# Two attention heads side by side, a recurrence that starts from the values, and state-space blocks in pairs: one change to a whole-model kernel

## The reference

```python
# first block, layer 0
m = silu(c) @ w_mod + b_mod                  # 6 D modulation terms from one vector
qkv = silu(depthwise_conv5(p))               # 4 heads of 128
# gated delta rule, forward and backward, over context and then latent tokens:
sol = triangular_solve(lower + eye, [v * b, k * b * exp(gcum)], unit_diagonal=True)
v_new = u - w @ state
state = state * exp(g_last) + k_tail.T @ v_new
o = q_dec @ state + intra @ v_new            # wanted for latent tokens only
# beside it, attention: 8 query heads and 2 key heads of 64, over 512 keys
p = softmax(q @ k.T * 64 ** -0.5); o_b = p @ v
y = concat([rms_norm(o) * silu(z), o_b]) @ w_out
h = h + gate * rms_norm(y);  h = h + gate * rms_norm(swiglu_ffn(h))
# layer 1: a conformer convolution of 31 taps, and a second swiglu_ffn
# second block: three branches of one projection
_, s = associative_scan(combine, (a_bar, B u))       # 32 groups, 64 complex states
y_a = gelu(Re(C s) + d * u);  y_a = y_a * sigmoid(y_a @ w_glu)
y_b = gate_b * causal_conv3(gate_c * x)
y_c = forgetting_attention(q, k, v)                  # 8 heads of 64, decay from f
x = x + rms_norm(sum(sigmoid(gate_i) * (y_i @ w_i)) @ w_out);  then a squared-relu FFN
```

## Time and profile before

| | |
|---|---|
| median of 3 runs | 1442.45 us (1440.03 to 1442.77) |
| the profiled execution | 1443.34 us, of it a span of 1441.4 |
| TensorE (PE) busy | 1338.2 us, 93% |
| VectorE (DVE) busy | 859.3 us, 60% |
| ScalarE (ACT) busy | 480.6 us, 33% |
| GpSimd (POOL) busy | 121.9 us, 8% |
| read from HBM | 223.81 MB, 156 GB/s over the span |

### The profile page before, as it was taken

One profiled execution on the slowest core, in us unless ns is written; L12 is line 12 of the kernel. 1 busy time (PEld: TensorE's weight loads), 2 busy tenths in 40 slices (PEclk: granted clock), 3 DMA queues, 4 the chain that ended last, 5 costly groups with the idle time before them and its releaser, 6 DMA issues.

```text
span 1441.4 us, 18815 instructions
## 1 busy us (share of the span) xinstructions
PE 1338.2 (93%) x7086; PEld 1000.3 (69%) x7086; DVE 859.3 (60%) x1542; ACT 480.6 (33%) x822; POOL 121.9 (8%) x169
## 2 busy tenths in 40 slices
PE   3899968986899999899999999799999999899997
PEld 1564645553488888687488888677777787588886
DVE  1106795443477767496777677378862242577776
ACT  2243235310343343302553443311213230444443
POOL 0041020000000000200000000244530000000000
PEclk9899978998999999899999999999999999999999
DMA  9221244786745553141445555123233233355541
GB/s 393 78 88 45 100 157 176 286 328 233 275 155 182 201 184 133 67 159 44 150 164 202 184 180 196 64 101 131 93 127 110 109 118 106 130 202 178 196 179 59
DMA packets 24655, 225.69 MB, mean 157 GB/s; under 512 B 2705, under 2 KB 2833, under 8 KB 4370
## 3 DMA queue, kind: packets, MB, share of 16 engines
q1 hardware_dynamic: 23040, 220.31, 41.7%
q10 hardware_dynamic: 1554, 4.56, 0.9%
HBM read 223.81 MB, written 1.05 MB: 156 GB/s over the span
## 4 chain that ended last, share of the span: by engine, by line
PE 84%; DVE 7%; DMA 4%; ACT 3%; issue 1%; ACTq 0%; DVEq 0%
PE psum L751 19%; PE psum L829 15%; PE psum L869 14%; PE psum L830 8%; PE psum L782 6%; PE psum L1382 3%; PE psum L914 3%; DMA ring<-in_w_mod 2%; PE psum L734 2%; DMA h<-in_x 2%; PE psum L942 2%; DVE arena L2119 1%; PE psum L1279 1%; PE psum L705 1%; PE psum L1293 1%
## 5 line engine op out<-in xcount | busy, mean ns | idle before, releaser
L829 PE MATMUL psum<-aT_r,arena_r 128*128 128x512 f32 x920 | 327.5, 398 | 0.5 <-DVE arena_r L2020 0.5
L2020 DVE TENSOR_TENSOR arena_r<-ring,arena_r 128x1024 fp32r<-128x1024 f32 x196 | 229.6, 1221 | 129.0 <-ACT arena_r L1489 129.0
L751 PE MATMUL psum<-aT,ring 128*128 128x256 f32 (+1 forms) x1216 | 303.7, 407 | 1.8 <-DVE aT L1983 1.8
L751 PEld LDWEIGHTS psum<-aT,ring 128*128 128x128 f32 x1216 | 229.1, 191 | 70.0 <-issue 42.4
L830 PE MATMUL psum<-aT_r,arena_r 128*128 128x256 f32 x920 | 258.2, 281 | 0.0
L1489 ACT ACTIVATE arena_r<-ring 128x1024 fp32r<-128x1024 f32 x196 | 194.7, 1050 | 161.3 <-PE psum L869 139.1
L869 PE MATMUL psum<-arena_r 128*128 128x512 f32 x912 | 221.9, 392 | 0.0
L829 PEld LDWEIGHTS psum<-aT_r,arena_r 128*128 128x128 f32 x920 | 172.8, 188 | 42.6 <-issue 0.7
L869 PEld LDWEIGHTS psum<-arena_r 128*128 128x128 f32 x912 | 165.9, 188 | 36.4 <-issue 0.3
L830 PEld LDWEIGHTS psum<-aT_r,arena_r 128*128 128x128 f32 x920 | 173.7, 189 | 2.7
L1501 ACT ACTIVATE nrm<-nrm 128x256 f32<-128x256 f32 x76 | 31.8, 418 | 171.1 <-DVE nrm L2034 171.1
(11 more groups left out here) (428 smaller groups left out, 1545.3 us busy)
## 6 DMA issues: line engine op xcount, KB each, us to landing
ring<-in_w_ffn SPq DMA_DIRECT2D x44, 1536.0 KB, 6.6
ring<-in_w_mod SPq DMA_DIRECT2D x32, 1536.0 KB, 7.4
ring<-in_w_ff SPq DMA_DIRECT2D x32, 1024.0 KB, 4.8
ring<-in_w_in_g SPq DMA_DIRECT2D x8, 1536.0 KB, 6.6
ring<-in_w_conf_i SPq DMA_DIRECT2D x8, 1024.0 KB, 4.7
ring<-in_w_hyb_f SPq DMA_DIRECT2D x4, 1536.0 KB, 6.6
ring<-in_w_in_a SPq DMA_DIRECT2D x4, 1536.0 KB, 6.3
ring<-in_w_in_b SPq DMA_DIRECT2D x4, 1536.0 KB, 6.7
```

The lines of the kernel that those rows point to most:

```text
L751: last = mm(bank(use)[:, out_at:out_at + rhs(k).shape[1]], weights[:, k * P:(k + 1) * P], rhs(k), start=(k == 0), stop=(k == KT - 1))
L829: mm(bank(use).rearrange("p (a t) -> p a t", a=2), hi, x_both[:, :, k, :], start=(k == 0), stop=False)
L2020: tt(w_lo[j % 2][:, at], slot(c)[:, at], w_hi[j % 2][:, at].bitcast(F32), ALU.subtract).then_inc(split_ready, 1)
```

## The change

**First attention.** Two heads that share 128 rows form a pair, and there are eight units (`NPAIR`). The two score products of a unit read the upper and the lower 64 rows and go to banks 0 and 1; VectorE takes both maxima in one instruction; the transposes come one unit later, not two; the outputs of both heads are issued in turn into the two column halves of one bank. `att_p` has six buffers, `att_pT` two places. `GAPS` becomes strings, worked from left to right (A: a unit, M: a chunk): one unit stands before the recurrence, the other nine turns in it.

**Ahead of the recurrence.** ScalarE takes both evictions of p5 and of p6, both of q6 and half the diagonal copies (those of GpSimd become four); VectorE keeps the second half of q5 and does the convolution of q behind it. `blocks_inverse` counts in two steps. The chain of v is worked before that of q. At s = 0 `vn` reads v itself, without a copy; q's transposes to tokens move behind the first `vn`, those back to features behind the second, the q by k products behind the second `ds`. `mod_take(2)` moves into the last step. The state S moves to another tile.

**Output projection.** `middle` is called after chunk 0.

**State-space stage.** `s5_in` and `s5_out` take two blocks at a time, their products in turn on neighbouring row groups and column groups. `s5_u` has banks 2 to 5, all projections banks 0 and 1, `s_ri` four buffers; `skip`, `gelu`, `glu_product`, `gated` and `forget` move by one or two places.

```diff
@@ -211,15 +211,16 @@
 USE["att_qk"] = BANKS.turn(3, (0, 1, 2))
 NATT = AH * TT
 USE["att_s"] = BANKS.turn(NATT, (0, 1))
-USE["att_t"] = BANKS.turn(NATT, (2,))
-USE["att_o"] = BANKS.turn(AH // 2, (3,))
-USE["p5"], USE["q5"] = beside(2), beside(2)
+USE["att_t"], USE["att_o"] = [], []
+NPAIR = NATT // 2
+for _n in range(NPAIR + 2):
+    if _n >= 3 and _n % 2:
+        USE["att_o"] += BANKS.turn(1, (3,))
+    if 1 <= _n <= NPAIR:
+        USE["att_t"] += BANKS.turn(2, (2, 3))
+USE["p5"], USE["q5"], USE["p6"] = beside(2), beside(2), beside(2)
 _v = beside(4)
-USE["p6"] = beside(2)
-USE["to_tok"] += beside(2) + _v
 USE["q6"] = beside(2)
-USE["to_feat"] += beside(2)
-USE["kq"] = beside(2)
 for _s in range(4):
     if _s:
         for _d in range(2):
@@ -227,6 +228,12 @@
     for _what in ("vn",) + ("os",) * (_s >= 2) + ("ds",) * (_s < 3) + ("oi",) * (_s >= 2):
         for _d in range(2):
             USE[_what, _s, _d] = beside(1)[0]
+        if (_s, _what) == (0, "vn"):
+            USE["to_tok"] += beside(2) + _v[2:] + _v[:2]
+        elif (_s, _what) == (1, "vn"):
+            USE["to_feat"] += beside(2)
+        elif (_s, _what) == (1, "ds"):
+            USE["kq"] = beside(2)
...
-USE["in_a"] = BANKS.turn(12)
-USE["in_v"] = BANKS.turn(4)
+USE["in_a"] = BANKS.turn(12, (0, 1))
+USE["in_v"] = BANKS.turn(4, (0, 1))

 USE["b_bar"] = BANKS.turn(2, (4, 5))
-USE["in_b"] = BANKS.turn(12)
-USE["in_g"] = BANKS.turn(24)
-USE["s5_u"] = BANKS.turn(S5T, (4, 5))
+USE["in_b"] = BANKS.turn(12, (0, 1))
+USE["in_g"] = BANKS.turn(24, (0, 1))
+USE["s5_u"] = BANKS.turn(S5T, (2, 3, 4, 5))
...
-FORGET = {7: 0, 9: 1, 11: 2, 13: 3, 14: 4, 15: 5}
+FORGET = {7: 0, 9: 1, 11: 2, 14: 3, 15: 4}
...
-    "qk": (2, 1), "p5": (1, 1), "q5": (1, 1), "p6": (1, 1), "q6": (1, 2),
-    "vn0": (2, 2), "ds0": (2, 2), "ks1": (2, 2), "vn1": (2, 2), "ds1": (2, 2),
-    "ks2": (1, 2), "vn2": (1, 2), "ds2": (1, 2), "ks3": (1, 2), "vn3": (0, 3),
+    "qk": "MAM", "p5": "M", "q5": "M", "p6": "M", "q6": "M", "vn0": "MAM", "ds0": "MAM", "ks1": "AM", "vn1": "MAM",
+    "ds1": "MAMM", "ks2": "MAM", "vn2": "MAM", "ds2": "MAM", "ks3": "MAMM", "vn3": "MMM",
 }
+SCAN_GAPS = [*GAPS][5:]
...
-        att_pT = view(ring, 1536, 2, 4, T)
-        att_p = view(ring, 3584, 3, 512)
+        att_p = view(ring, 0, 6, 512)
+        att_pT = [view(x, at, 2, 4, T) for x, at in ((ring, 3072), (arena, 10240))]
...
-        S = view(arena, 5120, 2, 512)
+        S = view(yT_t, 0, 2, 512)
...
-        s_ri = view(z_t, 0, 2, 2, T)
+        s_ri = [view(x, at, 2, T) for x, at0 in ((z_t, 0), (arena, 9768)) for at in (at0, at0 + 2 * T)]
...
-                    if middle and c == 1:
+                    if middle and c == 0:
...
+                for n in range(NPAIR + 2):
+                    if n < NPAIR:
+                        pair, t = n // 2, n % 2
+                        for half in range(2):
+                            wait_free(pe, USE["att_s"][2 * n + half])
+                        for half in range(2):
+                            use, q = USE["att_s"][2 * n + half], slice(64 * half, 64 * half + 64)
+                            filled(mm(bank(use), qbT[q, pair, t * P:(t + 1) * P], kbT[q, :], start=True, stop=True), use)
+                    if n >= 3 and n % 2:
+                        pair = (n - 3) // 2
+                        use = USE["att_o"][pair]
+                        for half in range(2):
+                            wait_read(pe, USE["att_t"][4 * pair + 2 + half])
                         wait_free(pe, use)
                         for kb in range(4):
+                            for half in range(2):
+                                q0 = 64 * half
+                                v = pctx[:, kb, 128 + q0:192 + q0] if kb < 2 else ptok[:, kb - 2, 640 + q0:704 + q0]
+                                last = mm(bank(use)[q0:q0 + 64, 0:T], v, att_pT[pair % 2][:, half, kb, :],
+                                          start=(kb == 0), stop=(kb == 3))
+                        filled(last, use)
+                    if 1 <= n <= NPAIR:
+                        m = n - 1
+                        pe.wait_ge(att_norm, n)
+                        for half in range(2):
+                            transposes(USE["att_t"][2 * m + half],
+                                       [att_p[:, 2 * (m % 3) + half, kb * P:(kb + 1) * P] for kb in range(4)])
                     yield
...
-                    n = 4 * d + ORDER[d][s]
-                    pe.wait_ge(resid_ready, 2 * s + d + 1)
+                    st = ORDER[d][s]
+                    if s:
+                        pe.wait_ge(resid_ready, 2 * (s - 1) + d + 1)
+                    else:
+                        wait_read(pe, USE["to_tok"][6 + st])
                     use = USE["vn", s, d]
                     wait_free(pe, use)
-                    filled(per_head(use, hs(XT, n), hs(r_st, d)), use)
+                    filled(per_head(use, hs(XT, 4 * d + st), hs(r_st, d) if s else hs(vtok, st)), use)
+                if s < 2:
+                    (q_tokens, q_features)[s]()
...
+                if s == 1:
+                    key_query()
...
+            def s5_in(p):
+
+                pair = (2 * p, 2 * p + 1)
+                for i in pair:
+                    wait_free(pe, USE["s5_u"][i])
                 for part in range(2):
+                    for i in pair:
+                        use, r0, blk = USE["s5_u"][i], 32 * (i % 4), i // 4
+                        last = mm(bank(use)[:, part * T:(part + 1) * T], bT[r0:r0 + 32, part, blk, :],
+                                  uT[r0:r0 + 32, blk, :], start=True, stop=True)
+                        if part:
+                            filled(last, use)
...
+            def s5_out(p):
+
+                pair, blk = (2 * p, 2 * p + 1), p // 2
+                pe.wait_ge(s5_state, 2 * p + 2)
                 use = USE["s5_y"][blk]
+                if p % 2 == 0:
                     wait_free(pe, use)
                 for part in range(2):
+                    for i in pair:
+                        r0 = 32 * (i % 4)
+                        last = mm(bank(use)[r0:r0 + 32, 0:T], c_bd[:, part, i, :], s_ri[i % 4][:, part, :],
+                                  start=(part == 0), stop=(part == 1))
+                if p % 2:
                     filled(last, use)
                 else:
                     last.then_inc(s5_part, 1)
...
             s5_in(0)
             for i in range(S5T):
                 next(filler)
-                if i + 1 < S5T:
-                    s5_in(i + 1)
+                if i % 2 == 0 and i + 2 < S5T:
+                    s5_in(i // 2 + 1)
                 for _ in range(BESIDE[i] - 1):
                     next(filler)
-                if i:
-                    s5_out(i - 1)
+                if i >= 3 and i % 2:
+                    s5_out(i // 2 - 1)
...
-            s5_out(S5T - 1)
+            s5_out(S5T // 2 - 1)
+            next(filler)
+            glu_product(2)
...
-                        v.tensor_copy(r_st[:, d, :], vtok[:, st, :]).then_inc(resid_ready, 1)
...
+                    unit_rows(4, 6, HD ** -0.5)
                 if s:
                     pause(f"ks{s}")
+                if s == 1:
+                    mod_take(1)
                 for d in range(2):
...
+                if s == 3:
+                    mod_take(2)
...
+                if s == 0:
+                    unit_sums(4, 6)
                 if s == 1:
+                    intra()
                     mod(0, (2, 3, 4, 5))
                     row_diag(0)
...
-            mod_take(2)
...
```

More of the change, by code:

```diff
@@ L1033, in attention @@
                     yield
             def pause(name):
[L1037 to L1042 removed]
+                for step in GAPS[name]:
+                    next(units if step == "A" else between, None)
             between, units = mods(), attention()
             pause("qk")
[L1046 removed]
+            pe.wait_ge(blocks_inverse, 2)
@@ new lines, in attention @@
+                    if n >= 3 and n % 2:
+                        pair = (n - 3) // 2
+                        use = USE["att_o"][pair]
+                        wait_full(act, use)
+                        freed(fn(yT[:, 4 + pair, :], bank(use)[:, 0:T], ACT.Copy), use)
+                    if 1 <= n <= NPAIR:
+                        m = n - 1
+                        for half in range(2):
+                            use = USE["att_t"][2 * m + half]
+                            wait_full(act, use)
+                            freed(fn(att_pT[m // 2 % 2][:, half, :, m % 2 * P:(m % 2 + 1) * P],
+                                     bank(use).rearrange("p (a b) -> p a b", a=4), ACT.Copy), use)
@@ L1684, in _, with unit_diagonals @@
-            act.wait_ge(blocks_inverse, 1)
-            use = USE["p5"][0]
-            wait_full(act, use)
-            freed(fn(blk_p[:, 0:16, :].rearrange("p a b -> p (a b)"), bank(use), ACT.Copy), use)
-            act.wait_ge(zeroed, 1)
-            for d in range(2):
```

(6 more changed lines are left out.)

304 lines of the change are left out of this document (126 added, 178 removed).

## The result

The changed kernel takes 1428.49 us (median of 8 runs, 1423.88 to 1433.93), the kernel before 1440.65 in the same series (1437.74 to 1442.77): a ratio of 0.9914, 95% interval 0.9892 to 0.9936. It is 12.2 us faster, where 31.5 were forecast; 1428.49 lies above the range of 1401 to 1425.

The account below looks back on a forecast made before the run. TensorE, holding 84% of the chain, was taken as the bound. From 1442.45 us, -21.5 (recurrence and ahead of it), +3 (output projection) and -13 (state-space stage) summed to -31.5: 1411 us, range 1401 to 1425.

Parts of the forecast that it names:

- v's first product at 222: Ahead of the recurrence: v's first use comes at about 222 against 246.7, 24.5 us earlier.
- The same pace gives 326.8: Recurrence: 19 chunks at 5.2 us apiece put the last chunk product at 326.8, against 348.3 before: -21.5 us.
- Rival B: Recurrence: TensorE stands for the attention's scaling in most steps; first term -10, total -20, 1422 us; chance 0.15.
- Two of my signs: Recurrence, signs of being right: last chunk issue near 320, not 341.6; over 15 us of waits for in_w_mod.
- The limit stays TensorE, by 4 us: State-space loop: VectorE ends near 1059, TensorE wants its last state near 1063, so TensorE still sets the end.
- My sign for being wrong: State-space loop: VectorE never idle and TensorE waiting for its states would show the forecast wrong; no size given.
- The output projection, +3: Output projection: the feature step after chunk 0 delays ffn0's first loads by 3.4 us; +3, bounds 0 and +3.4.
- The halves side by side: Attention and state-space products on different row or column groups overlap; an s5 pair costs 1.1 and 1.0 us.
- rival C: Recurrence and state-space stage: the halves don't run side by side; total -7.5, 1435 us; chance 0.06.
- Projections on two banks: State-space stage: projections get two banks in place of four; cost 0, up to +3 if ScalarE stands at gelu.
- Rival D: Recurrence runs at the lower clock as TensorE waits for transfers; if held throughout, +48, 1490 us; chance 0.05.
- the bounds I had given myself, -5 and -6: Least gains allowed: -5 for the recurrence term forecast at -21.5, -6 for the state-space term forecast at -13.

Follow-up runs that it names:

- four edits: Changed kernel with a modulation product moved into gap ks1, ScalarE's output copy before the exponentials, cum_k one place later, middle after chunk 1: 1408.91 us, ratio 0.9768.
- three edits: Changed kernel with a modulation product moved into gap ks1, cum_k products one place later, middle after chunk 1: 1409.61 us, ratio 0.9786.

## Why the prediction was wrong

**v's first product at 222:** the number was met (222.7), partly by luck. The p6 products were to start at 207.9 and started at 212.5, behind the pause of 5.3 us that was in no sum of mine; the way from there to v took 10.2 us, where I had summed 14.3, since the transposes, both chunk products and q6 ran at the high level (2.0, 1.5 and 2.1, not 3.1, 2.8 and 3.1). Where the pause was short, v came ahead of my 220: seven of thirteen profiles lie between 215.5 and 219.5. The wait for q's SiLU, 3.3 against 3, and the first chunk product in the steps, 229.4 against 228, were right.

**"The same pace gives 326.8":** this step failed. I gave all 19 turns 5.2 us. Measured, from 229.4: three turns of 4.4, one of 17.8, fifteen of 5.05 (336.1 in all). The mean pace was right; one turn was not a turn of the slots. I counted the M's of the gaps as chunks and priced the attention's waits in one lump of 3 us, without laying out what stands between one product and the next. Placed, the same waits cost more: in that stretch they came on top of each other, one of them (bank 3, freed by ScalarE behind two exponentials) was in no sum of mine, and the low clock behind them added 1.7 at the `vn` products. Rival B, TensorE standing for the scaled attention, was the nearest in kind, and its first term of -10 nearer than mine to the 12.2 measured, but it spread its price over most steps: what costs is the long stretch and, less, the turn of 8.8. Two of my signs failed with this step: the last chunk's load is issued at 327.6, not near 320, and the waits for these loads sum to 13.6 us, not to over 15.

**"The limit stays TensorE, by 4 us":** this failed as well. Pairs cost what was forecast: 1.13 and 1.06 against 1.1 and 1.0, TensorE has its 15 us, and the 1.9 at the branch products came as forecast (1.85). The comparison of totals came out the other way, if by little: from its first block to its last state VectorE took 119.1 us, not 117, to 1048.9, and TensorE, without the wait, would have come for that state at about 1048, a little ahead of it and not 4 behind; with `cum_k` moved it stands 1.5 for it. My sign for being wrong, VectorE never idle in the loop and TensorE waiting for its states, is met. That costs 1.5, though, and the miss is 8: I compared only ends. Between them TensorE's lead grows, and `cum_k(1)`, in order, waits for a piece of VectorE's program whose place I had seen move (`FORGET`, 13 to 14) and had not priced: 8.1, and 1.3 for the clock at the two blocks behind it. The second attention therefore starts 4.0 sooner, counted from the first projection block (159.2 behind it, not 163.2), not 11 to 12: 8 short. With `cum_k` one place later the whole stage gives 14.2 (247.0 to 232.8), more than the 13 forecast.

**The output projection, +3:** right (+3.4). The first split stood 22.5 behind the projection's start before (378.3 less 355.8), 26.2 after:

```profile
369.01 2.95 ACT L1518 ACTIVATE arena_r<-ring 128x1024 fp32r<-128x1024 f32 x3 [15.83 <-DMA ring<-in_w_ffn]
```

**The halves side by side:** right, rival C falls. A pair of scores takes 1.13 where one took 1.12. For the state-space products, s5_in before and after stand on L1279 and L1302:

```profile
L1279 PE MATMUL psum<-arena,tok 32*128 32x256 f32 x61 | 17.3, 400 | 0.0
L1302 PE MATMUL psum<-arena,tok 32*128 32x256 f32 x64 | 9.1, 400 | 0.8 <-ACT tok L1863 0.8
```

A call of one block took 17.3 / 61 x 4 = 1.13 us, a call of a pair takes 9.1 / 64 x 8 = 1.14, and s5_out 16.8 and 8.4 us for its 64 records: 2.0 times. That is not the 1.54 that I had estimated from the figure for four row tiles in the Trainium skill, "TensorE: Matmul & The Clock Gate", section "Part 3: Packing small matmuls".

**Projections on two banks:** no wait for them is seen; right.

**Rival D:** the clock was 0.86 in the first 37.6 us and 0.96 after, not held low; a small part of it is in the long stretch.

The range failed because both misses had one sign and the lower gains of each term were not added: with the bounds I had given myself, -5 and -6, the sum would have been -7.6, 1435. The four edits, which take out what the two failed steps had overlooked, bring the kernel to 1408.9, where 1411 was forecast: the last chunk product 20.5 sooner against 21.5, nothing in place of +3 at the output projection, 14.2 against 13 in the state-space stage. That agreement belongs to another kernel than the one predicted.

## What to carry to other kernels

Where engines work in order, compare them at every hand-over, not at the end of a stage: making one faster turns each product that waits for the other's program into a candidate, and moving it by one place may give back the whole wait. With a ring of two slots, find the longest stretch between two of its products, and take work and waits out of that one; 7 us of the same work behind it cost at most a few us here, as long as it made no other turn long. A wait shared by way of a PSUM bank doesn't show in the code of either user: list, for each bank, who frees it and what stands ahead of that.

## What the hardware showed beyond what I had expected

Removing a wait of 2.4 us shortened the stretch by 5.4, since the products behind it ran at the high level again (2.03 and 0.75 against 3.76 and 1.33). The level behind such a wait isn't the same each time: with the chunk product in ks1, waits of 0.78 and 2.43 stand ahead of it, and the products behind them ran at the high level (chunk 1.50, `vn` 2.05); with three edits, the same recurrence and waits of 0.93 and 2.43, they took 2.79 and 2.89.

Products on different row or column groups ran side by side whether issued in turn or block by block: 8 records in 1.13 and 1.14 us, as 4 records of one block before (1.13). The Trainium skill, "TensorE: Matmul & The Clock Gate", section "Part 3: Packing small matmuls", says that matmuls start strictly in program order. The records of the run with pairs block by block don't agree with it: the semaphore of the first block's last product is counted by the seventh record of eight, and the second block's first record starts 0.01 us behind the first. The measurement decides for this form, if the chip got the products in the order of the code; neither that nor the reason is shown by a run here.

One kernel's executions spread over 10 us (1423.88 to 1433.93) with mean clocks of 0.956 to 0.966, and a stage that no edit touched took 235.1 or 237.9 us. A profile of one execution can flatter a kernel by 3 us, and that of the chunk product in ks1 did by 4.9; the gain of an edit is better read from its stage in the profile and from medians together.
